# Seven products for the second block's FFN: weight sums by adding DMAs, a new order of the turns, and SiLU as one ScalarE function

## The reference, cut to what matters

```python
hn = rmsnorm_2(h, ffn_norm_g)
ff = jax.nn.silu(jnp.einsum('bld,df->blf', hn, w_gate)) * jnp.einsum('bld,df->blf', hn, w_up)
return h + jnp.einsum('blf,fd->bld', ff, w_down)
```

## Time and profile before

| | us |
|---|---|
| median of 3 runs | 3521.31 |
| lowest and highest | 3519.25, 3524.53 |
| the profiled execution's own time | 3520.74 |
| its span | 3518.9 |
| TensorE busy in the span | 3138.5 |
| VectorE, ScalarE, POOL busy | 2119.6, 1283.7, 551.4 |

### The profile page before, as it was taken

One profiled execution on the slowest core, in us unless ns is written; L12 is line 12 of the kernel. 1 busy time (PEld: TensorE's weight loads), 2 busy tenths in 40 slices (PEclk: granted clock), 3 DMA queues, 4 the chain that ended last, 5 costly groups with the idle time before them and its releaser, 6 DMA issues. The chain is left out here.

```text
span 3518.9 us, 52575 instructions
## 1 busy us (share of the span) xinstructions
PE 3138.5 (89%) x19600; PEld 2788.4 (79%) x19600; DVE 2119.6 (60%) x3378; ACT 1283.7 (36%) x2147; POOL 551.4 (16%) x444
## 2 busy tenths in 40 slices
PE   3999799999997998999989998779788998778887
PEld 2678778888885787888879878779788987677785
DVE  7558676546555685544444456776854346785774
ACT  3343633323223444444443323432333322443332
POOL 0000210110111002112230002322311000430421
PEclk8999899999998998999989999889999999889988
DMA  6231123223222311222221111212222111212212
GB/s 250 70 111 60 44 89 132 103 100 120 107 95 85 116 55 37 85 90 90 95 85 49 49 45 53 71 63 93 72 80 95 43 49 49 72 60 80 88 66 90
DMA packets 105701, 288.76 MB, mean 82 GB/s; under 512 B 36272, under 2 KB 36400, under 8 KB 104272
## 3 DMA queue, kind: packets, MB, share of 16 engines
q1 hardware_dynamic: 100304, 269.73, 22.8%
q0 software_dynamic: 3808, 10.38, 0.9%
q10 hardware_dynamic: 1440, 6.62, 0.5%
HBM read 284.56 MB, written 2.10 MB: 81 GB/s over the span
## 5 line engine op out<-in xcount | busy, mean ns | idle before, releaser
L343 PE MATMUL ps<-h_hi,hi_ring 128*128 128x512 f32 (+2 forms) x2672 | 872.4, 326 | 65.5 <-DVE h_lo L716 42.2
L343 PE MATMUL ps<-h_lo,hi_ring 128*128 128x512 f32 (+2 forms) x2672 | 843.6, 316 | 0.0
L343 PE MATMUL ps<-h_hi,lo_ring 128*128 128x512 f32 (+2 forms) x2672 | 840.4, 315 | 0.0
L270 DVE TENSOR_TENSOR lo_ring<-ring,hi_ring 128x1024 fp32r<-128x1024 f32 (+1 forms) x322 | 378.9, 1178 | 666.7 <-ACT hi_ring L260 665.2
L343 PEld LDWEIGHTS ps<-h_hi,hi_ring 128*128 128x128 f32 x2672 | 513.9, 192 | 127.4 <-issue 82.5
L260 ACT ACTIVATE hi_ring<-ring 128x1024 fp32r<-128x1024 f32 (+1 forms) x322 | 326.2, 1015 | 719.7 <-PE ps L343 673.4
L343 PEld LDWEIGHTS ps<-h_lo,hi_ring 128*128 128x128 f32 x2672 | 514.9, 193 | 33.6 <-issue 3.9
L343 PEld LDWEIGHTS ps<-h_hi,lo_ring 128*128 128x128 f32 x2672 | 512.3, 192 | 30.8
L2402 PE MATMUL ps<-ffn_operand,hi_ring 128*128 128x264 f32 (+1 forms) x704 | 167.9, 337 | 137.4 <-DVE arena L3421 125.2
L343 PE MATMUL ps<-hid_hi,hi_ring 128*128 128x512 f32 (+1 forms) x768 | 275.6, 359 | 3.3 <-DVE hid_lo L1087 3.3
L343 PE MATMUL ps<-hid_lo,hi_ring 128*128 128x512 f32 (+1 forms) x768 | 275.0, 358 | 0.0
(11 more groups left out here) (401 smaller groups left out, 5937.2 us busy)
## 6 DMA issues: line engine op xcount, KB each, us to landing
ring<-weights_dram SPq DMA_DIRECT2D x334, 512.0 KB, 3.3
mod_ring<-w_mod_dram SPq DMA_DIRECT2D x64, 512.0 KB, 4.4
ring<-weights_dram SPq DMA_DIRECT2D x76, 384.0 KB, 3.0
arena<-w_mod_dram SPq DMA_DIRECT2D x48, 512.0 KB, 3.4
x<-x_dram SPq DMA_DIRECT2D x1, 3072.0 KB, 16.7
arena<-c_rows_dram ACTq DMA_DIRECT2D x3, 1024.0 KB, 6.5
arena<-ret_decay_dram POOLq DMA_DIRECT2D x2, 1056.0 KB, 6.2
silu_rows<-c_rows_dram ACTq DMA_DIRECT2D x2, 1024.0 KB, 5.3
```

The source lines that it names most:

```text
L270: self.nc.vector.tensor_tensor(self.lo_ring[:, g % SPLIT, 0:w], self.ring[:, g % RING, 0:w], self.hi_ring[:, g % SPLIT, 0:w], ALU.subtract ...
L343: ins = nc.tensor.matmul(out[0:m, c:c + n], w, a[:, t0:t0 + n], start=first and k == 0 and p == 0, stop=last and k == kts - 1 and p == 2)
```

## The change

*Sums.* POOL adds nothing more itself. It issues four DMAs a turn that read a quarter of the weights from DRAM again and add it to a quarter that already lies in the ring: A22 on A21 (sum 1), A21 on A11 (sum 3), A11 on the sum in A21's place (sum 2), and A12 on that (sum 6). Each overwrites its quarter, so it waits until the low part of the operand that lay there before is made: sum 3 for operand 0, sum 2 for operand 1, sum 6 for operand 2. Sum 1 waits for the second block's load. The four are counted by a semaphore each, and the high part of the operand waits for its own. `w_sums` is gone.

*Places and order.* Operands 4 and 5 (A12 and A22) are split in one instruction of 1024 columns; it takes one slot of the split rings, and operands 3 and 6 take the other. Operand 6 is now split in its own turn. `core.done` is counted by products 5 and 6, `core.lo` by the splits of 4 and 6. VectorE's order in a turn becomes: low parts 0 and 1 of the next turn, low part 6 of this one, L3421's operation, the hidden low part of the turn before, the operations of L3425, L3428 and L3432, low parts 2 and 3, those of L3435, L3438 and L3440, low part 4 (with 5), the product with the up half. ScalarE's becomes: the bank copy, the hidden copy of the turn before, high parts 0, 1, 6, 2, 3, 4 (with 5), the function of the gate. The first turn of a side is written out ahead of the loop on both engines, on both sides.

*Gate.* ScalarE's function is Silu, and VectorE's product of sigmoid and gate is gone.

```diff
-RAW, SUMS = {0: (0, 0), 4: (0, 1), 5: (1, 1)}, {1: 0, 2: 1, 3: 2, 6: 3}
+A11, A12, A21, A22 = (0, 0), (0, 1), (1, 0), (1, 1)
+SOURCE = {0: A11, 1: A21, 2: A21, 3: A11, 6: A21}
+SUMS = {1: (A21, A22), 3: (A11, A21), 2: (A21, A11), 6: (A21, A12)}
...
+    def split(self, p, q):
+
+        if q != 4:
+            return self.ring(p, *SOURCE[q]), *self.operand(p, q)
+        first = 0 if self.turned_over(p) else (self.g0 + 2 * p) % RING
+        step = RING - 1 if self.turned_over(p) else 1
+        both = lambda ap: ap[:, self.g0 % SPLIT, :].rearrange("p (a n) -> p a n", a=2)
+        return self.core.ring[:, first:first + step + 1:step, HALF:BLOCK], both(self.core.hi_ring), both(self.core.lo_ring)
...
-    def add_weights(self, pool, t, n, p):
...
-        tt(sums[:, 0, :], ring(1, 0), ring(1, 1), ALU.add).then_inc(self.made.sem, 1)
...
-        tt(sums[:, 1, :], sums[:, 0, :], ring(0, 0), ALU.add).then_inc(self.made.sem, 1)
...
-        tt(sums[:, 2, :], ring(0, 0), ring(1, 0), ALU.add).then_inc(self.made.sem, 1)
...
-        tt(sums[:, 3, :], sums[:, 1, :], ring(0, 1), ALU.add).then_inc(self.made.sem, 1)
+    def add(self, pool, n, p, q):
+
+        core, (at, added) = self.core, SUMS[q]
+        if q == 1:
+            self.landed(pool, 0, p, 1)
+        else:
+            pool.wait_ge(self.lo.sem, self.lo.at(4 * n + {3: 0, 2: 1, 6: 2}[q] + 1))
+        block, k_half = added
+        source = core.dram["weights"][core.order[self.g0 + 2 * p + block], :, k_half * HALF:(k_half + 1) * HALF]
+        pool.dma_start(self.ring(p, *at), source, accum_op=ALU.add).then_inc(self.made[q].sem, 16)
...
     def part_hi(self, act, t, n, p, q):
 
         core = self.core
-        if q in RAW:
-            self.landed(act, t, p, RAW[q][0])
+        if q in (0, 4):
+            self.landed(act, t, p, 0)
+            if q:
+                self.landed(act, t, p, 1)
         else:
-            act.wait_ge(self.made.sem, t * 8 + self.made.at(4 * n + SUMS[q] + 1))
-        if p:
-            if q in (4, 6):
-                act.wait_ge(core.done, t * 4 + self.g0 + 2 * (p - 1) + (1 if q == 4 else 2))
-            else:
-                act.wait_ge(self.product.sem, t * 10 + self.product.at(5 * (n - 1) + min(q, 4) + 1))
-        elif q >= 3:
-            act.wait_ge(core.done, self.g0 - SPLIT + (q - 3) // 2 + 1)
+            act.wait_ge(self.made[q].sem, t * 32 + self.made[q].at(16 * (n + 1)))
+        if q in (4, 6):
+            free = self.g0 + 2 * (p - 1) + (1 if q == 4 else 2)
+            act.wait_ge(core.done, t * 4 + free)
+        elif q == 3 and not p:
+            act.wait_ge(core.done, self.g0)
         elif n:
-            act.wait_ge(self.product.sem, self.product.at(5 * (n - 1) + q + 1))
+            act.wait_ge(self.product.sem, t * 10 + self.product.at(5 * (n - 1) + q + 1))
...
             for m in range(KT):
                 sq.add(pool, sqt, m)
-                if m == 3:
-                    sides[0].add_weights(pool, 0, 0, 0)
+                for q in {4: (1,), 5: (3, 2), 6: (6,)}.get(m, ()):
+                    sides[0].add(pool, 0, 0, q)
             for i, side in enumerate(sides):
-                if i:
-                    side.add_weights(pool, 0, H_TILES, 0)
-                tiles(pool, H_TILES - 1, 2, lambda t, n: side.add_weights(pool, t, i * H_TILES + n + 1, n + 1))
+                for p in range(H_TILES):
+                    for q in (3, 2, 6) if i or p else ():
+                        side.add(pool, i * H_TILES + p, p, q)
+                    if p < H_TILES - 1:
+                        side.add(pool, i * H_TILES + p + 1, p + 1, 1)
+                    elif not i:
+                        sides[1].add(pool, H_TILES, 0, 1)
...
-                for q in ((0, 1, 2), (3, 4), (5, 6))[i - last_block + 2] if i >= last_block - 2 else ():
+                for q in ((0, 1), (2,), (3, 4))[i - last_block + 2] if i >= last_block - 2 else ():
...
+                def hidden_hi(t, i):
+                    act.wait_ge(product_ready.sem, t * 2 + product_ready.at(n0 + i + 1))
+                    nc.scalar.activation(hid[:, t * 2 + i, 0, 0:tokens], up_f[:, 0:tokens], ACT.Copy
+                                         ).then_inc(hid_done.sem, 1)
+
+                def pair(t, i, start=False, final=False):
                     following = lambda q: seven.part_hi(act, t, n0 + i + 1, i + 1, q)
                     seven.came(act, t, n0 + i, i, 0)
                     nc.scalar.activation(taken[:, 2, 0:width], seven.bank(i, 0), ACT.Copy).then_inc(seven.copied.sem, 1)
-                    for q in range(0 if final else 6):
-                        following(q)
+                    if not start:
+                        hidden_hi(t, i - 1)
+                    if not final:
+                        following(0)
+                        following(1)
+                    seven.part_hi(act, t, n0 + i, i, 6)
+                    if not final:
+                        following(2)
+                        following(3)
+                        following(4)
                     act.wait_ge(taken_in.sem, t * 2 + taken_in.at(n0 + i + 1))
-                    nc.scalar.activation(sig_f[:, 0:tokens], gate_f[:, 0:tokens], ACT.Sigmoid).then_inc(sigmoid.sem, 1)
+                    nc.scalar.activation(sig_f[:, 0:tokens], gate_f[:, 0:tokens], ACT.Silu).then_inc(sigmoid.sem, 1)
...
-                tiles(act, H_TILES - 1, 2, pair)
-                pair(0, H_TILES - 1, True)
+                pair(0, 0, start=True)
+                tiles(act, H_TILES - 2, 2, lambda t, i: pair(t, i + 1))
+                pair(0, H_TILES - 1, final=True)
...
                     following(0)
                     following(1)
+                    seven.part_lo(dve, t, n, i, 6)
                     seven.came(dve, t, n, i, 2)
                     dve.wait_ge(seven.copied.sem, t * 2 + seven.copied.at(n + 1))
                     took(v.tensor_tensor(second, seven.bank(i, 1), taken[:, 2, 0:width], ALU.subtract))
-                    following(2)
+                    if not start:
+                        hidden_lo(t, i - 1)
                     seven.came(dve, t, n, i, 3)
                     own(1)
                     took(v.tensor_tensor(third, seven.bank(i, 3), second, ALU.add))
-                    following(3)
+                    if not start:
+                        dve.wait_ge(hid_ready.sem, t * 2 + hid_ready.at(n))
                     own(2)
                     took(v.tensor_tensor(u2, third, seven.bank(i, 2), ALU.subtract))
...
                     took(v.tensor_tensor(g1, seven.bank(i, 0), r1, ALU.mult))
-                    following(4)
+                    following(2)
+                    following(3)
                     seven.came(dve, t, n, i, 5)
                     took(v.tensor_tensor(u1, seven.bank(i, 3), second, ALU.add))
-                    following(5)
                     seven.came(dve, t, n, i, 6)
                     took(v.tensor_tensor(g2, seven.bank(i, 2), second, ALU.subtract))
                     own(6)
                     v.tensor_tensor(g2, g2, r2, ALU.mult).then_inc(taken_in.sem, 1)
-                    following(6)
+                    following(4)
+                    dve.wait_ge(sigmoid.sem, t * 2 + sigmoid.at(n + 1))
+                    v.tensor_tensor(u, u, sg, ALU.mult).then_inc(product_ready.sem, 1)
...
-                    dve.wait_ge(sigmoid.sem, t * 2 + sigmoid.at(n + 1))
-                    v.tensor_tensor(sg, sg, g, ALU.mult).then_inc(gated.sem, 1)
-                    dve.wait_ge(gated.sem, t * 2 + gated.at(n + 1))
-                    v.tensor_tensor(u, u, sg, ALU.mult).then_inc(product_ready.sem, 1)
-                    dve.wait_ge(hid_done.sem, t * 2 + hid_done.at(n + 1))
-                    v.tensor_tensor(hid[:, t * 2 + i, 1, 0:tokens], u, hid[:, t * 2 + i, 0, 0:tokens], ALU.subtract
-                                    ).then_inc(hid_ready.sem, 1)
```

More of the change, by code:

```diff
@@ L2309, in landed, with turned_over, operand @@
         eng.wait_ge(self.core.landed[g % RING], t * 16 + 16 * (g // RING + 1))
-    def operand(self, q):
+    def turned_over(self, p):
+        return (self.g0 + 2 * p) % RING == RING - 1
+    def operand(self, p, q):
         if q < 3:
             return self.extra[:, q, 0, :], self.extra[:, q, 1, :]
-        slot, part = (self.g0 + (q - 3) // 2) % SPLIT, (q - 3) % 2
+        slot, part = (self.g0 + (q in (3, 6))) % SPLIT, q == 6 or q in (4, 5) and (q == 5) != self.turned_over(p)
         cols = slice(part * HALF, (part + 1) * HALF)
@@ L2366, in part_hi @@
+        source, hi, _ = self.split(p, q)
+        ins = core.nc.scalar.activation(hi, source, ACT.Copy)
+        if q < 4:
             ins.then_inc(self.hi.sem, 1)
@@ L2368, in part_hi, with split_ready @@
             ins.then_inc(core.hi, 1)
+    def split_ready(self, eng, t, n, p, q, count, blocks):
+        if q < 4:
+            eng.wait_ge(count.sem, t * 8 + count.at(4 * n + q + 1))
+        else:
```

(32 more changed lines are left out.)

56 lines of the change are left out of this document (18 added, 38 removed).

## The result

The changed kernel takes 3564.45 us (median of 4 runs, 3558.68 to 3570.52) against 3520.28 us (3515.96 to 3524.53) before: a ratio of 1.0126, 95% interval 1.0104 to 1.0148. Forecast were 3455 us and a range up to 3560. The profiled execution took 3566.78 us with a span of 3564.8, 45.9 more than before's 3518.9.

What follows compares the result with a forecast made beforehand. TensorE's wait for VectorE's evacuation of the second bank was taken to bound turns of 15.24 us. Cutting 36 turns to 13.35 saves 68 us, edges +2.8 - 4.6: 3520.7 - 66 = 3455 us, range 3395 to 3560.

Steps and rivals of the forecast that it cites:

- Step 1: Gate: dropping VectorE's product takes 0.70 us off its late chain; table loads should leave the loop, costed at nothing.
- the ring: Dependence loop each turn: issue sum 6, sum 1 lands, operand 1 split, sum 2 lands, operand 2 split; period 13.35 us.
- Step 2: POOL's four additions go, and with them the 0.96 us they add to each VectorE instruction hit.
- Step 3: New order of a turn without the DMAs: 10.8 us, or 12.3 if TensorE's low clock stays for 15 matmuls.
- Step 4: POOL's adding DMAs set the pace: a turn takes 3.35 us plus the landings of sums 1 and 2, 13.35 together.
- L1 = L2 = 5.0: Landing times in us of sums 1 and 2, taken from a 264 KB load behind an equal one, 5.1 rounded.
- Step 5: SP's weight loads come early enough that nothing waits for them: cover 1.5 us.
- Step 6: Edges of the up-stage sides: side 1 starts 2.3 us later, 4.6 lost in all; four last turns win 2.8.
- C: Rival, chance 0.24: slower, landings from 5.95 us each make turns longer than today's; 3541 at 6.2, 3597 at 7.
- A: Rival, chance 0.24: landings are short and TensorE's chain decides, turns of 12.3 us, 3417; 3363 without the low clock.
- B: Rival, chance 0.09: landings of 5.6 to 5.9 us eat nearly all the gain, 3498 to 3519 us.
- D: Rival, chance 0.03: ScalarE's table loads come into every turn, +1.3 us each, hence 3502 us.

Runs made afterwards that it cites:

- e4: Kernel before with Silu as one function and VectorE's product of sigmoid and gate taken out, nothing else: 3446.39 us, ratio 0.9789.
- e11: Changed kernel with POOL's additions restored, low part 4 behind the up product and the second bank's evacuation ahead of low part 6: 3377.20 us, ratio 0.9589.
- e8: Changed kernel with the old gate, Sigmoid on ScalarE and the product on VectorE: 3572.57 us, ratio 1.0155 to the kernel before.
- e2: Changed kernel with its four adding DMAs as plain copies of the same size, sums left out: 3393.55 us, ratio 0.9642 to the kernel before.
- e3: Changed kernel with POOL's four additions into w_sums restored in place of the adding DMAs: 3442.45 us, ratio 0.9773 to the kernel before.
- e6: Changed kernel with POOL's additions restored and VectorE's low part 4 moved behind the up product: 3399.91 us, ratio 0.9667 to the kernel before.
- e5: Changed kernel with SyncE's up-stage weight loads bringing only half of each block, 256 KB for 512 KB: 3514.03 us, ratio 0.999 to the kernel before.
- e10: Changed kernel with the load into the slot freed by low part 6 held until sum 2 has landed: 3516.44 us, ratio 0.9987 to the kernel before.
- e1: Changed kernel with POOL's queue in the order 3, 2, 1 of the next turn, 6: 3496.55 us, ratio 0.9932 to the kernel before.
- e7: Changed kernel with sum 1 issued ahead of sum 6, and sum 2 ahead of sum 3: 3499.84 us, ratio 0.9947 to the kernel before.

## Why the prediction was wrong, point by point

- **What bounds the kernel now: right.** e4 and e11 shorten exactly that wait, to 71.9 and 36.5 us.
- **Step 1, the gate: right in the changed kernel by luck of place, mis-sized as an edit.** Its 0.70 lies off the ring; e8 was 8 us slower, with intervals that overlap. On the kernel before it is worth 73, since an instruction of VectorE moves out of POOL's addition. I had priced the product and the hits in separate steps and had not asked how they meet. No table load is left inside the loops, as forecast. Silu isn't what takes them out: e4 still has them (1.28 at 2257.33 and 2266.66), and e8, with Sigmoid, has none. The first turn written out ahead is the likely cause, but no run has it alone.
- **Step 2: right.** VectorE's splits of 512 columns take 0.69 now, for up to 1.65, and the one of 1024 takes 1.22, as forecast.
- **Step 3, the order without the DMAs: not contradicted, and not measured by itself.** Forecast were 10.8 to 12.3 a turn. With copies it is 12.2, with landings still in the chain (e2). With POOL's additions in their place it is 13.3 (e3), and 12.1 and 11.6 once one and two instructions of VectorE are moved (e6, e11).
- **Step 4, the failed step: the term "L1 = L2 = 5.0".** The ring closes where I put it, with the same two waits in it, and its length is the sum that I wrote down. But the landings are 6.2 and 6.1 (12.26 for 10.0), and the fixed part is 4.16 for 3.35: each hand-over from VectorE to POOL takes 0.3, where I had 0.07 for both, and ScalarE starts 0.1 behind each landing, which I had left out. The 0.58 between the two issues was right (0.62). 36 x 2.26 = 81 us and 36 x 0.81 = 29 us make the 111 us between turns of 13.35 and 16.43. I took the landings from a plain load, and wrote that this left "nothing for the second read that an addition must make". e2 shows the addition to be the largest item: 1.66 us of the engines for 0.82, and landings of 12.3 in sum for 7.5. The page "Collectives: The Full Stack" of the Trainium skill (Part 3, on the fold count) says that an addition in the DMA needs two source reads; the engine time of e2 agrees with it (twice a copy's), and it spoke against the change. The bytes that the profile counts don't show a second read.
- **Step 5, SP's loads: wrong.** I checked whether the load comes too late for its own reader, which it doesn't, and cost its traffic at "a little". What it does is to start with sum 2 in every turn, since low part 6 frees its slot as low part 1 releases the sum, and the other load starts 2.2 behind sum 1 in most turns. Together that is some 50 us (e5, e10).
- **Step 6, edges: right in kind, small in size.** Side 1 starts 5.6 us late in each layer for the 2.3 forecast; side 0 starts 6.1 and 2.9 early, which I had at nothing; the last turns lose 1.5 in place of winning 2.8.
- **The rivals.** C happened: at landings of 6.2 and 6.1 its formula gives 15.6, its price line 3541 for 6.2 each; the rest is the fixed part. The sign hung on 5.95 and I gave that side 0.23. A's time (3417) is near what copies gave (3393.55), B's is where the kernel stands with the loads out of the way (e5, e10) or the ring open (e1): 3497 to 3516. D didn't happen.
- **What would show it.** I had named landings over 6 as what would make me wrong; they are 6.2 and 6.1 on the ring, though the page's median over all four places is 4.9, which would have passed as my 5.0. Only the landings by place decide.

Left open: how much of sum 1's 6.2 is the sum ahead of it, how much the load behind it, and how much POOL's own work for an issue. In e10, where sum 1 goes out 1.9 us behind sum 6, it lands in 5.3 (mean, 3.9 to 7.2), but the loads are elsewhere there too. In e1, with no other sum just ahead of it and no load within 3 us behind it, it lands in 3.9.

## What to carry to other kernels

Before moving an addition into the DMA, write down the chain of landings that depend on one another in one turn, price each with an adding DMA of that size at its own place on the queue, and look at what else the same event releases: here the release of a buffer started a 512 KB load beside the very transfer that everything waited for. A median over all places hides this. And where two engines hit each other, an edit is worth its own duration plus or minus the hits that it moves: time the parts of such a change separately, for the best kernel here is the change without its adding DMAs, with two of VectorE's instructions moved.

## What the runs showed of the hardware that I had not expected

- An adding DMA of 256 KB occupies the sixteen engines for 1.66 us, a plain copy for 0.82, at equal counted bytes and 144 for 80 packets; POOL's issue takes 0.875 us for 0.536, and the shortest landing in one stretch was 3.7 us for 2.8.
- Of two adding DMAs issued 0.5 to 0.6 us apart, the second landed in 6.2 to 7.0 us (means: sum 1 in the changed kernel, sum 2 in e1, sum 3 in e7). The first landed in 4.0 and 4.4 where a 512 KB load started 2.7 and 1.1 behind it, and in 6.1 where one started 0.5 behind it (e7).
- One addition of POOL stretches a VectorE instruction that starts during it by about 1 us (0.69 to 1.65, and 1.22 to 2.32 for 1024 columns in e3). One that starts 0.16 us before it keeps its 0.70 (e4, in all 36 regular turns).
